# A third seven-product weight unit in two down projections of a two-block transformer

## What is computed

```python
h = rms_norm(x, norm_ffn_g[l])
u = causal_depthwise_conv(h @ ffn_w_up[l], ffn_conv_w[l], ffn_conv_b[l])   # 256 x 5632, 3 taps
x = x + (silu(u[..., :2816]) * u[..., 2816:]) @ ffn_w_down[l]             # 256 x 2816 @ 2816 x 1024
```

## Time and profile before

| | |
|---|---|
| median of three runs | 1215.99 us |
| profiled execution, first to last instruction | 1214.1 us |
| TensorE (matmul) busy | 1205.5 us, 99% |
| VectorE busy | 903.9 us, 74% |
| ScalarE busy | 671.1 us, 55% |
| granted TensorE clock, mean | 0.999 of full speed |
| down projections of the second block's feed-forwards | 860.1 to about 919 us, and 1149.7 to 1208 us |

### The profile page before, as it was taken

One profiled execution on the slowest core, in us unless ns is written; L12 is line 12 of the kernel. 1 busy time (PEld: TensorE's weight loads), 2 busy tenths in 40 slices (PEclk: granted clock), 3 DMA queues, 4 the chain that ended last, 5 costly groups with the idle time before them and its releaser, 6 DMA issues.

```text
span 1214.1 us, 17930 instructions
## 1 busy us (share of the span) xinstructions
PE 1205.5 (99%) x7099; PEld 1048.0 (86%) x7099; DVE 903.9 (74%) x1105; ACT 671.1 (55%) x807; POOL 51.3 (4%) x101
## 2 busy tenths in 40 slices
PE   9999999999999999999999999999999999999998
PEld 7888888888899888888888889999888888999986
DVE  5566465568886685566988986988887998698886
ACT  7655354445466664444648556555655755566553
POOL 2000000000010000000010020000001011000000
PEclk9999999999999999999999999999999999999999
DMA  9644645545654335554555454455574435555550
GB/s 349 232 164 168 223 147 200 194 163 196 243 191 166 131 141 206 207 179 168 193 214 174 139 177 161 152 205 174 174 262 161 140 107 184 191 179 180 196 196 35
DMA packets 32568, 220.40 MB, mean 182 GB/s; under 512 B 3888, under 2 KB 4048, under 8 KB 6768
## 3 DMA queue, kind: packets, MB, share of 16 engines
q1 hardware_dynamic: 29888, 212.33, 49.3%
q0 software_dynamic: 1664, 5.41, 1.3%
q10 hardware_dynamic: 944, 1.64, 0.4%
HBM read 218.31 MB, written 1.05 MB: 181 GB/s over the span
## 4 chain that ended last, share of the span: by engine, by line
PE 92%; DVE 6%; DMA 1%; issue 0%; POOL 0%; ACT 0%; ACTq 0%; POOLq 0%; DVEq 0%
PE acc L1850 20%; PE acc L1852 20%; PE acc L1851 20%; PE tb L1878 3%; PE tb L2521 3%; PE tb L2520 3%; PE acc L2520 3%; PE acc L2521 3%; PE tb L2518 3%; PE acc L2518 3%; DVE cacc L1534 3%; DVE wlo L1143 1%; PE acc L2158 1%; PE acc L2160 1%; PE acc L2161 1%; PE tb L1850 1%
## 5 line engine op out<-in xcount | busy, mean ns | idle before, releaser
L1143 DVE TENSOR_TENSOR wlo<-raw,whi 128x2048 fp32r<-128x2048 f32 x184 | 417.3, 2287 | 131.8 <-ACT whi L592 131.8
L592 ACT ACTIVATE whi<-raw 128x2048 fp32r<-128x2048 f32 (+1 forms) x198 | 368.4, 1882 | 56.5 <-PE acc L1852 43.9
L1850 PE MATMUL acc<-whi,xth 128*128 128x512 f32 x704 | 279.8, 397 | 0.6 <-DVE xtl L1241 0.5
L1852 PE MATMUL acc<-whi,xtl 128*128 128x512 f32 x704 | 274.7, 390 | 0.0
L1851 PE MATMUL acc<-wlo,xth 128*128 128x512 f32 x704 | 274.3, 390 | 0.0
L1850 PE MATMUL acc<-whi,yth 128*128 128x512 f32 (+1 forms) x428 | 169.0, 395 | 0.0
L1852 PE MATMUL acc<-whi,ytl 128*128 128x512 f32 (+1 forms) x428 | 166.6, 389 | 0.0
L1851 PE MATMUL acc<-wlo,yth 128*128 128x512 f32 (+1 forms) x428 | 166.4, 389 | 0.0
L1850 PEld LDWEIGHTS acc<-whi,xth 128*128 128x128 f32 x704 | 132.3, 188 | 28.0 <-DVE wlo L1232 1.3
L1852 PEld LDWEIGHTS acc<-whi,xtl 128*128 128x128 f32 x704 | 132.2, 188 | 28.1
L1851 PEld LDWEIGHTS acc<-wlo,xth 128*128 128x128 f32 x704 | 132.4, 188 | 25.7
(11 more groups left out here) (407 smaller groups left out, 1919.3 us busy)
## 6 DMA issues: line engine op xcount, KB each, us to landing
raw<-in_stream SPq DMA_DIRECT2D x200, 1024.0 KB, 5.0
rb<-in_rel_rows POOLq DMA_DIRECT2D x8, 256.0 KB, 2.9
x<-in_x_in ACTq DMA_DIRECT2D x4, 256.0 KB, 7.4
raw<-in_stream SPq DMA_DIRECT2D x2, 512.0 KB, 9.3
gs_sb<-in_gs_row POOLq DMA_DIRECT2D x1, 1024.0 KB, 7.6
frow<-in_fin_row POOLq DMA_DIRECT2D x2, 512.0 KB, 6.0
raw<-in_stream SPq DMA_DIRECT2D x2, 256.0 KB, 7.0
ws_sb<-in_ws_t POOLq DMA_DIRECT2D x1, 512.0 KB, 7.7
```

The lines of the kernel that those rows point to most:

```text
L592: act.activation(whi[:, s, c0:UNIT], raw[:, s, c0:UNIT], ACT.Copy).then_inc(hi_ready, 1)
L1143: dve.tensor_tensor(wlo[:, s, :], raw[:, s, :], whi[:, s, :], ALU.subtract).then_inc(lo_ready, 1)
L1850: pe.matmul(o, xh, wh, start=first, stop=False)
L1852: return pe.matmul(o, xl, wh, start=False, stop=last)
```

## The change

`FSEVEN_POS` goes from (6, 8) to (4, 6, 8): in both layers unit 4 of the down projection is also done with seven block products. The sums' buffers move: `fsum` (now three sets) and `fusum` go to where the normed input `xth`, `xtl` of the first three up steps lay, and the first weight-sum buffer goes from there to where the up projection's scratch `us` and `cv` lay. Semaphore counts follow.

```diff
-FSEVEN_POS = (6, 8)
+FSEVEN_POS = (4, 6, 8)
+FSEVEN = 3
...
-        fsum = at("fsum", [2 * 3 * P], o_sc)
-        fsum_l = at("fsum_l", [2 * 3 * P], o_sc, F32R)
-        fsum_h = at("fsum_h", [2 * 3 * P], o_sc + 2 * 3 * P, F32R)
-        fwsum_at = (o_xh, o_sc + 5120)
+        fsum = at("fsum", [FSEVEN * 3 * P], o_xh)
+        fsum_l = at("fsum_l", [FSEVEN * 3 * P], o_xh, F32R)
+        fsum_h = at("fsum_h", [FSEVEN * 3 * P], o_xh + FSEVEN * 3 * P, F32R)
+        fwsum_at = (o_sc, o_sc + 5120)
...
-        fusum = at("fusum", [3, 512], o_sc + 2048)
+        fusum = at("fusum", [3, 512], o_xh + 2 * FSEVEN * 3 * P)
...
         def y_hi_count(e, n):
-            return 3 + 13 * min(e, 2) + 5 * max(e - 2, 0) + n
+            return 3 + 13 * min(e, 2) + (2 * FSEVEN + 1) * max(e - 2, 0) + n
...
         def made_count(e, n):
-            return 2 + 36 * min(e, 2) + 22 * max(e - 2, 0) + n
+            return 2 + 36 * min(e, 2) + (7 * FSEVEN + 8) * max(e - 2, 0) + n
...
-                    if j == FSEVEN_POS[1] + 4:
+                    if j == FSEVEN_POS[-1] + 4:
                         first_sum(2 + l)
...
-                    dve.wait_ge(unit_used, down_at(e) + (SEVEN_POS[i - 2] + 1 if i >= 2 else 0))
+                    dve.wait_ge(unit_used, down_at(e) + (sevens(e)[i - 2] + 1 if i >= 2 else 0))
...
-                dve.wait_ge(side_made, made_count(2 + l, 7 * 2 + 8))
+                dve.wait_ge(side_made, made_count(2 + l, 7 * FSEVEN + 8))
```

More of the change, by code:

```diff
@@ L380, in y_hi_count @@
         def y_hi_count(e, n):
-            return 3 + 13 * min(e, 2) + 5 * max(e - 2, 0) + n
+            return 3 + 13 * min(e, 2) + (2 * FSEVEN + 1) * max(e - 2, 0) + n
         def w_hi_count(e, n):
-            return y_hi_count(e, (8 if e < 2 else 2) + n)
+            return y_hi_count(e, (8 if e < 2 else FSEVEN) + n)
         def y_lo_count(e, n):
-            return 3 + 8 * min(e, 2) + 4 * max(e - 2, 0) + n
+            return 3 + 8 * min(e, 2) + 2 * FSEVEN * max(e - 2, 0) + n
         def made_count(e, n):
-            return 2 + 36 * min(e, 2) + 22 * max(e - 2, 0) + n
+            return 2 + 36 * min(e, 2) + (7 * FSEVEN + 8) * max(e - 2, 0) + n
         def is_seven(U):
@@ L1986, in out_product @@
                         if c == 768:
-                            pe.wait_ge(side_made, made_count(3, 7 * 2 + 8))
+                            pe.wait_ge(side_made, made_count(3, 7 * FSEVEN + 8))
                         for j in (n - 2, n - 1):
```

## The result

| | before | after |
|---|---|---|
| median | 1215.99 us (1215.35 to 1216.23, 5 runs) | 1222.47 us (1220.44 to 1223.02, 5 runs) |
| ratio | | 1.0049, 95% interval 1.0037 to 1.0061 |
| span of the profiled execution | 1214.1 us | 1221.1 us |
| mean granted clock, run by run | 0.999 to 1.000 | 0.997, 0.998, 0.998 in the runs of 1222.81, 1222.47 and 1223.02; 0.999 in those of 1220.96 and 1220.44 |

Slower by 6.5 us; 5.1 were forecast, and the range was 1217.8 to 1223.2. The profiled execution is one of the slower three (1222.81).

What follows compares the result with a forecast made beforehand. TensorE bounds the kernel (99% busy), but its suppliers lag some 15 us at unit 4. Waits of 3.23 less 0.68 saved, over two layers, give +5.1: span 1219.2, runs 1221.1 us; range 1217.8 to 1223.2.

Steps and rivals of the forecast that it cites:

- Three matmuls less are 0.68 a layer: Unit 4 of the down projection: three matmuls removed at 0.227 each save 0.68 us a layer, 1.36 in two.
- The activation sums shift VectorE by 1.46 and nothing gives it back: Up projection: step 4's added sums lengthen one VectorE pass by 1.46 us, and everything following is that much later.
- `lo_ready` at 882.50 and `sums_lo` done at 886.90: Layer 0, unit 4: VectorE's weight sums end at 882.50, and the sums' low part at 886.90.
- A restart costs 0.22: TensorE after each wait at unit 4: late start and wider first matmul distance add 0.22 us.
- Waits of 0.87 and 2.36, none at units 6 and 8: Unit 4, each layer: TensorE waits for VectorE 0.87 and 2.36 us, together 3.23; only unit 4 is late.
- Moved buffers cost nothing: New places of the sums' buffers are written only after their old users are through, so no wait is added.
- The clock rival: TensorE's idling at unit 4 brings back the slow clock for nine matmuls: 2.2 us a layer, 1225.4; chance 0.07.
- No wait: Unit 4's `sums_lo` is done by 884.5, so TensorE sees no wait: 1214.6 us; chance 0.07.
- shift absorbed: Up projection absorbs the activation sums' delay, so only 1.77 us of wait a layer remains: 1218.2 us; chance 0.10.
- Later units covered by 1.6, unit 9 at 910.2: Layer 0 after unit 4: VectorE's work for unit 6 is ready 1.6 us early; unit 9 begins at 910.2, not 907.69.

Runs made afterwards that it cites:

- experiment 8: Changed kernel with ScalarE and VectorE reordered in the up projection loop, preparing the next pass's first unit earlier: 1214.54 us, ratio 0.9990 to the kernel before.
- experiment 1: Kernel before, with the activation sums of up step 4 also made but not used: 1215.95 us, ratio 0.9998.
- experiment 5: Changed kernel where unit 4's `lo` signals TensorE itself, in place of the last weight sum: 1224.08 us, ratio 1.0067 to the kernel before.
- experiment 3: Changed kernel's buffers, but only two seven-product units, at positions 5 and 8: 1216.02 us, ratio 1.0003 to the kernel before.
- experiment 4: Changed kernel with 3 and 9 useless matmuls put before TensorE's two waits at unit 4: 1220.84 us, ratio 1.0040 to the kernel before.
- experiment 7: Kernel before, with ScalarE and VectorE reordered in the up projection loop, preparing the next pass's first unit earlier: 1216.02 us, ratio 1.0001.
- experiment 2: Changed kernel's buffers, but only two seven-product units, at positions 4 and 8: 1219.42 us, ratio 1.0028 to the kernel before.

## Why the prediction was right

- *Three matmuls less are 0.68 a layer.* Right, but seen bare only in experiment 8: 0.68 in layer 0, and 1.24 of 1.36 in the median.
- *The activation sums shift VectorE by 1.46 and nothing gives it back.* Right, 1.48 (12.32 and 12.33 for pass 6, forecast 12.31; experiment 1).
- *`lo_ready` at 882.50 and `sums_lo` done at 886.90.* Measured 882.74 and 887.14, of which 0.16 to 0.18 is the shift of the trace.
- *A restart costs 0.22.* Measured 0.16: the matmul starts 0.05 and 0.06 behind the end of VectorE's instruction (882.74 to 882.79, 887.14 to 887.20), not 0.15 as in the opening, and the wider first distance adds 0.11 and not 0.07. The 0.06 too much was made up at the first wait by `lo_ready`, which came some 0.07 later than reckoned.
- *Waits of 0.87 and 2.36, none at units 6 and 8.* Measured 0.89 and 2.32, none. I wrote them as two terms of a sum. Experiment 5 shows that they hang together: the end of `sums_lo` against the time at which p5 is asked for. The sum was right because it was taken along the chain.
- *Moved buffers cost nothing.* Shown by experiment 3, to within 0.12%.
- *The clock rival, 0.07, 2.2 us a layer, 1225.4.* This is the step that was weighed wrongly. It happened in three of the five runs, if the two without a trace are read by their clock and time, and in one layer there (1.59 in the profiled run, where I had priced 2.2); in the profiled run of experiment 5 it happened in both. I had a price from the opening, where nothing but the spacing showed it, and no wait of 2 us to read in this trace; from that I concluded a small chance, where the honest reading was that the trace didn't say. The price was too high as well: it was 9 matmuls with 0.24 more each, and eight came, 0.425 apart, 0.20 more each. The two runs with a clock of 0.999, 1220.44 and 1220.96, are what the sum of 1221.1 stood for; the median of 1222.47 is that plus one drop. So the mechanism of the sum held (2.60 a layer measured for its 2.55), and the rest of the 6.5 us is a term that the sum put at nothing. That the median still lies in the range is partly luck: a drop in both layers gives about 1224 (experiment 5).

  What speaks for the waits as the cause of the drops: filled waits (experiment 4) none in five runs, one longer wait (5) a lower clock in each of five, and in all ten traces the clock is down behind such waits alone. It isn't proof: the groups are small, and one run in 65 of the kernel before (1217.84) and one in 11 of experiment 3 (1218.19) had the time and clock of a drop (0.998), though the traces of these kernels show no such wait.

  The Trainium skill, page "TensorE: Matmul & The Clock Gate", section on HAM oscillation, says that idle gaps bring the throttled state back. The runs agree, though its example has gaps of 3 to 5 us and the longest here was 2.96.
- *No wait* and *shift absorbed* fell, by the view of waits and by experiment 1.
- *Later units covered by 1.6, unit 9 at 910.2.* Right: no wait there, and 910.45, of which 0.16 is the shift.

## What to carry to other kernels

A stage in which the busiest engine never waits says nothing of how late its suppliers are; lay the supplier's end against the first instant at which its product is asked for, and spend no cover that isn't there. When two waits of one engine hang on one chain of another, taking away the earlier gains nothing; here one longer wait even cost 1.6 us more than two short ones, by the clock. Before taking work from the bound engine, look for idle time in the suppliers' own mutual waits: here an order that gained nothing by itself (experiment 7) was what turned a loss of 6.5 us into a gain of 1.2.

## What the runs showed of the hardware that I had not expected

- After waits of 0.6 and 2.0 us of idle time, 4 us apart, the granted clock fell to half in layer 1 and not in layer 0 of the same execution, about 1 us after matmuls had begun again. It was back after eight matmuls. With one wait of 2.95 us a layer it fell in both, in the profiled run. With a wait of 1.5 us a layer (experiment 2, eight runs) no run had a granted clock under 0.999. The changed kernel's time came in two groups 2 us apart, where the kernel before scatters by 0.9 in its first five runs (in the later comparisons one run of it in 60 lay well outside, at 1217.84).
- A restart after a wait costs a second small sum: the first matmul's distance to the next was 0.34 and 0.33 in place of 0.23. It was 0.34 in experiment 4 too (887.22 - 886.88), where the idle time had been filled.
